# A hybrid decoder layer in fp32 on one core: the gate weights' split kept in DRAM by the first block of tokens and loaded by the other three

## What is computed

```
mod = silu(c) @ W_ada + b_ada              -> shift, scale, gate for two sub-layers
h   = RMSNorm(x) * (1 + scale1) + shift1
proj = h @ W_in    (attention q,k,v | DeltaNet q,k,v | beta | decay | out gate z | branch gate A | branch gate B)
A   = sliding-window attention (window 128, 8 heads, 2 kv heads, QK norm, partial rotary, sinks)
B   = gated DeltaNet (4 heads of 128, short conv, chunked triangular inverse, running state)
merged = sigmoid(gA) * (A @ W_branch[A]) + sigmoid(gB) * (B @ W_branch[B])
x   = x + gate1 * (merged @ W_out)
x   = x + gate2 * SwiGLU(RMSNorm(x) * (1 + scale2) + shift2)     hidden width 2816
```

## Time and profile before

| | |
|---|---|
| median of 3 runs | 3077.72 us (3077.09 to 3078.48) |
| profiled execution | 3072.56 us, its span 3070.8 us |
| busy VectorE | 1632.6 us, 53% |
| busy ScalarE | 1202.7 us, 39% |
| busy GpSimd | 113.2 us, 4% |
| moved | 358.22 MB, mean 117 GB/s |
| SP's queue | 33.8% of the 16 DMA engines' span |
| ScalarE's queue | 8.39 MB, 0.7% |

### The profile page before, as it was taken

How to read it: one execution, slowest core, us unless ns; L and a number is a source line. 1 busy time by engine, 2 the same in 40 slices (tenths; PEclk the granted TensorE clock), 3 DMA queues, 4 the chain that set the end, 5 groups by cost and what they waited for, 6 DMA issues and landing times.

```text
span 3070.8 us, 40245 instructions
## 1 busy us (share of the span) xinstructions
PE 3012.7 (98%) x16056; PEld 2526.0 (82%) x16056; DVE 1632.6 (53%) x2636; ACT 1202.7 (39%) x1969; POOL 113.2 (4%) x109
## 2 busy tenths in 40 slices
PE   7999999999999999999999999999999999999999
PEld 6897878888898788888889878888888978878887
DVE  7876675433566667333365756633336475643333
ACT  3555533222355544222234545422224455432222
POOL 0011000000001100000000110000000011000000
PEclk9999999999999999999999999999999999999999
DMA  6533343222433333222233244322233333322223
GB/s 255 186 127 93 134 162 146 96 96 98 135 111 113 105 129 116 98 103 96 96 131 124 95 118 142 103 96 96 96 100 134 125 110 100 124 82 96 96 96 103
DMA packets 137146, 358.22 MB, mean 117 GB/s; under 512 B 38144, under 2 KB 38272, under 8 KB 135040
## 3 DMA queue, kind: packets, MB, share of 16 engines
q1 hardware_dynamic: 132608, 347.27, 33.8%
q10 hardware_dynamic: 4352, 8.39, 0.7%
HBM read 326.25 MB, written 29.36 MB: 116 GB/s over the span
## 4 chain that ended last, share of the span: by engine, by line
PE 82%; DVE 8%; issue 4%; ACT 2%; DVEq 2%; DMA 1%; SPq 1%; POOL 0%; POOLq 0%; ACTq 0%
PE gb L1702 64%; PE gb L1719 7%; PE gb L2028 4%; PE mb L1873 2%; DVE tmp_c L1412 1%; DVE inv_c L1415 1%; DVE w_lo L1132 1%; PE mb L1846 1%; ACT sc L912 1%; DVE ada_sum L1123 1%; PE mb L1868 1%; PE mb L1788 1%; ACT sc L904 1%; DVE n_acc L1139 1%; DVE nf L1151 1%
## 5 line engine op out<-in xcount | busy, mean ns | idle before, releaser
L740 ACT ACTIVATE w_hi<-w_raw 128x1024 fp32r<-128x1024 f32 x492 | 518.8, 1057 | 1053.5 <-PE gb L1702 977.4
L1702 PE MATMUL gb<-h_hi,w_hi 128*128 128x512 f32 x2336 | 918.7, 393 | 12.0 <-DVE w_lo L1132 6.6
L1702 PE MATMUL gb<-h_lo,w_hi 128*128 128x512 f32 x2336 | 917.9, 393 | 0.0
L1702 PE MATMUL gb<-h_hi,w_lo 128*128 128x512 f32 x2336 | 917.7, 393 | 0.0
L1132 DVE TENSOR_TENSOR w_lo<-w_raw,w_hi 128x1024 fp32r<-128x1024 f32 x492 | 600.8, 1222 | 491.7 <-ACT w_hi L740 490.3
L1702 PEld LDWEIGHTS gb<-h_hi,w_hi 128*128 128x128 f32 x2336 | 440.5, 189 | 103.5 <-DVE w_lo L1132 8.3
L1702 PEld LDWEIGHTS gb<-h_lo,w_hi 128*128 128x128 f32 x2336 | 440.7, 189 | 96.0 <-issue 6.5
L1702 PEld LDWEIGHTS gb<-h_hi,w_lo 128*128 128x128 f32 x2336 | 440.3, 188 | 91.6
L1702 PE MATMUL gb<-hid_hi,w_hi 128*128 128x512 f32 x704 | 274.0, 389 | 0.0
L1702 PE MATMUL gb<-hid_hi,w_lo 128*128 128x512 f32 x704 | 273.9, 389 | 0.0
L1702 PE MATMUL gb<-hid_lo,w_hi 128*128 128x512 f32 x704 | 273.9, 389 | 0.0
(11 more groups left out here) (268 smaller groups left out, 3446.8 us busy)
## 6 DMA issues: line engine op xcount, KB each, us to landing
w_raw<-in_wstream SPq DMA_DIRECT2D x492, 512.0 KB, 3.2
ada_buf<-in_ada_w SPq DMA_DIRECT2D x9, 2048.0 KB, 8.3
x<-in_x SPq DMA_DIRECT2D x4, 2048.0 KB, 10.0
out<-x ACTq DMA_DIRECT2D x16, 512.0 KB, 2.9
ada_buf<-in_ada_w SPq DMA_DIRECT2D x6, 1024.0 KB, 14.8
xs<-in_x SPq DMA_DIRECT2D x12, 512.0 KB, 5.5
scratch_nt<-st_nt SPq DMA_DIRECT2D x16, 256.0 KB, 2.4
scratch_at<-st_at SPq DMA_DIRECT2D x16, 256.0 KB, 2.9
```

The lines of the kernel that those rows point to most:

```text
L740: act.activation(w_hi[s][:, :], w_raw[s][:, :], ACT.Copy).then_inc(w_high.sem, 1)
L1702: last = pe.matmul(bank(j), w, r, start=(i == 0), stop=(i == n - 1))
```

## The change

In block 0 the gate units are split as before, and after VectorE's half is done ScalarE stores the pair (hi, lo; 1 MB) to a DRAM tensor, at the start of its split of the next unit. In blocks 1 to 3 the gate units are neither loaded raw nor split: ScalarE, in the place of its split, waits for the slot and issues the load of the kept pair straight into `w_hi`/`w_lo`; VectorE skips them, and TensorE waits for that load. All other units are split as before; their counts are recomputed. w_hi[s] and w_lo[s] become the halves of one tile.

```diff
+def is_kept(g):
+    b, u = divmod(g, U_PER)
+    return 0 < b < NB and U_GATE <= u < U_BRANCH
+def splits(g):
+    return sum(not is_kept(i) for i in range(min(g, len(UNITS))))
+def loads(g):
+    return sum(not is_kept(i) for i in range(g % RING, g, RING))
+def same_place(g):
+    return max(i for i in range(g % RING, g, RING) if not is_kept(i))
+def kept_loads(g):
+    return sum(is_kept(i) for i in range(g % RING, g + 1, RING))
...
-    w_hi = [sb(f"w_hi{s}", [P, UW], fp32r) for s in range(RING)]
-    w_lo = [sb(f"w_lo{s}", [P, UW], fp32r) for s in range(RING)]
+    w_pair = [sb(f"w_pair{s}", [P, 2, UW], fp32r) for s in range(RING)]
+    w_hi, w_lo = [[w_pair[s][:, i, :] for s in range(RING)] for i in range(2)]
...
+    kept = nc.dram_tensor("scratch_w", (2 * KD, P, 2, UW), fp32, kind="Internal").ap()
...
+    w_kept = [sig(f"w_kept{s}", 0) for s in range(RING)]
+    kept_in = [sig(f"kept_in{s}", 0) for s in range(RING)]
...
             def load_unit(b, u):
-                sp.wait_ge(w_ready.sem, b * U_PER + (u + 1))
+                g = b * U_PER + u
+                if is_kept(g):
+                    return
+                sp.wait_ge(w_ready.sem, RING + splits(same_place(g) + 1))
...
+            def keep_unit(u):
+                s = u % RING
+                act.wait_ge(w_ready.sem, RING + u + 1)
+                act.dma_start(kept[u - U_GATE], w_pair[s][:, :, :].bitcast(fp32)).then_inc(w_kept[s].sem, 16)
...
             def split(b, u):
-                s = u % RING
-                if b * U_PER + u >= NB * U_PER:
+                s, g = u % RING, b * U_PER + u
+                if g >= NB * U_PER:
                     return
-                act.wait_ge(w_loaded[s].sem, b * w_loaded[s].per + 16 * (u // RING + 1))
+                if b == 0 and U_GATE < u <= U_BRANCH:
+                    keep_unit(u - 1)
                 unit_used(b, u - RING)
+                if is_kept(g):
+                    if b == 1 and u < U_GATE + RING:
+                        act.wait_ge(w_kept[s].sem, 16 * len(range(U_GATE + (s - U_GATE) % RING, U_BRANCH, RING)))
+                    act.dma_start(w_pair[s][:, :, :].bitcast(fp32), kept[u - U_GATE]).then_inc(kept_in[s].sem, 16)
+                    return
+                act.wait_ge(w_loaded[s].sem, 16 * (loads(g) + 1))
+                if b == 0 and U_GATE + RING <= u < U_BRANCH + RING:
+                    act.wait_ge(w_kept[s].sem, 16 * len(range(U_GATE + (s - U_GATE) % RING, u, RING)))
                 act.activation(w_hi[s][:, :], w_raw[s][:, :], ACT.Copy).then_inc(w_high.sem, 1)
...
             def split(b, u):
                 s = u % RING
-                if b * U_PER + u >= NB * U_PER:
+                g = b * U_PER + u
+                if g >= NB * U_PER or is_kept(g):
                     return
-                dve.wait_ge(w_high.sem, b * U_PER + (u + 1))
+                dve.wait_ge(w_high.sem, splits(g + 1))
...
+            def wait_weights(b, u):
+                g = b * U_PER + u
+                if is_kept(g):
+                    pe.wait_ge(kept_in[u % RING].sem, 16 * kept_loads(g))
+                else:
+                    pe.wait_ge(w_ready.sem, RING + splits(g + 1))
...
-                    pe.wait_ge(w_ready.sem, w_ready.at(b, u + 1))
+                    wait_weights(b, u)
```

## The result

The changed kernel takes **3095.44 us** (3095.05 to 3097.4, 4 runs) beside 3077.4 (3072.83 to 3078.48) for the kernel before on the same chip: a ratio of 1.0063, 95% interval 1.0051 to 1.0076, 18 us slower. The forecast was 3075.1, within 3068 to 3083.

A forecast was written before the change was run, and what follows sets the result against it. TensorE's own time, nearly the whole span, was taken as the bound. Terms: -1.5 (blocks 1 to 3), -2.1 (merge), +1.8 (block 0), -0.8 (clock) = -2.6 us; 3077.7 - 2.6 = 3075.1, range 3068 to 3083.

The forecast's parts named there:

- What bounds it, and the place: TensorE's time is nearly the whole span; only its waits and lower clock, beside attention and DeltaNet, can be won.
- Splits removed: Blocks 1 to 3: without VectorE's splits of units 6 and 7, the triangular sweeps end 1.8 us earlier.
- Unit 8 and the other units: Gate units: a 1 MB load takes 4.9 us; unit 8's wait nearly goes, the others land before use, costing nothing.
- The image chain against the new loads: Blocks 1 to 3: loads of units 9 and 10 meet image writes and `lc_u`; fair sharing costs 1.3 us, bounds 0 and 6.8.
- The rival on the slower side: `lc_u` before L1888, all four blocks: 1 MB loads go ahead of the images; 3090 to 3097 us; chance 0.13.
- one and a half transfers: The slower rival's case of 5 us of transfers ahead of the images in each block: +12.5 us, 3090.
- Clock, -0.8 us: Lower-clock falls of 1.7 and 1.5 us follow TensorE's waits in blocks 1 and 2; half of one was counted as won.
- signs of being wrong: L1888 waits of 5 us and more or below 2, L1702 waits on kept pairs, or a lower clock in new stretches.
- Block 0, +1.8: Block 0: stores of units 8 and 9 meet the image, 1.3 us, plus 0.5; bounds 0 and 6.8 + 1.5.
- the merge's 0.5: Block 0: ScalarE waits for unit 9, VectorE's rotation and merge come 1.5 us late, 1.0 covered by the later image.
- the ScalarE wait: Block 0: ScalarE waits for VectorE's split, exponentials(1,0) 2.5 us late; TensorE stands 0.9 there, 0.9 less for unit 8.
- The merge, -2.1: TensorE's waits of 1.3 and 0.8 us for VectorE's merge (L1427) go, as splits of units 8 to 10 leave: -2.1 us.

The follow-up runs named there:

- e1: The changed kernel, but gate units 9 and 10 split as before in blocks 1 to 3: 3078.58 us, 1.0006 to the kernel before.
- e10: The changed kernel with only gate unit 9 split as before in blocks 1 to 3: 3089.1 us, 1.0043 to the kernel before.
- e11: The changed kernel with only gate unit 10 split as before in blocks 1 to 3: 3088.51 us, 1.0042 to the kernel before.
- e6: The changed kernel with the kept tensor laid out in runs of 1 KB in DRAM instead of 8 KB: 3098.42 us, 1.0071 to the kernel before.
- e4: The changed kernel, all pairs kept, loads of units 8 and 9 earlier, 10 later, block 0's stores of 4, 6, 8, 9 later: 3070.95 us, 0.9983.
- e7: e4 with unit 10's load behind keep_qk(2) and 10 gate matmuls moved to just ahead of level_x(0): 3064.14 us, 0.996 to the kernel before.
- e2: The changed kernel with block 0 storing all pairs but nothing loaded, blocks 1 to 3 splitting all units: 3084.7 us, 1.0023 to the kernel before.
- e5: The changed kernel with the kept tensor laid out in runs of 4 KB in DRAM instead of 8 KB: 3096.19 us, 1.0064 to the kernel before.

## Why the prediction was wrong

**What bounds it, and the place** were right: the gain and the loss were decided between the last sweep and the first level product.

**Splits removed: right.** In block 1 the sweeps end 1.77 us earlier; 1.76 was forecast.

**Unit 8 and the other units: right in effect.** No wait for a kept pair, though a load takes 6.4 us and not 4.9. It was issued earlier than I had it (below). TensorE arrives 2.6 us earlier at the image, not 1.7.

**"The image chain against the new loads", 1.3 us: this is the step that failed.** It measured 4.4 us a block, 2.2 for each transfer (e1, e10, e11). The fair sharing that it assumed did not take place: 20 packets of SP's queue passed in 2.5 us beside the load, 1353 without it. I had read the DMA share of 0.41 as room, and shared the bandwidth fairly between `lc_u` and one load; the load of unit 9 against the image *writes* I had priced with nothing but an issue. The writes' own bandwidth was no measure: they stood still behind the load, SP's issues were stretched, and the chain is made of 17 of them end to end, which I had read from the earlier trace rows myself. Both loads also went out earlier than I had placed them and so met the writes: unit 9 beside the transpose and not behind it, 2.1 us earlier; unit 10 15.3 us after the copy of the scores, where 18.2 was forecast. With both my bounds in hand (0 and 6.8) I went near the lower one for the weight load that had left SP's queue behind `lc_u`. It was worth 0.5 us at most: from the issue of `lc_u` to the level product it is 4.0 us before and 3.6 in e1, where that load is gone too.

**The rival on the slower side** named this place and its price: it decided from 3.4 us a block, 4.4 were measured, and its formula gives 4 x 4.4 - 7.5 = +10.1 us of waits, beside +9.2 read from the trace. It was given 0.13. That its "one and a half transfers", 3090, come near the measured 3095 is in part luck: it has 5 us a block and nothing for the clock. The rule of the Trainium skill ("DMA: Bandwidth & Descriptors", Queues, rings and completion order: turns by whole packets of some 9 to 17 descriptors) spoke for it. A load here is 8 runs of 8 KB on each engine, which by this rule is one turn. The changed kernel agrees (the writes stood behind whole loads). e6 has 64 runs on each engine; by the typical size that is several turns, though the same section puts the ceiling of a packet at 64 descriptors, by which it would still be about one. More writes did get in beside one of its loads (590 packets, above), and the wait was no shorter.

**Clock, -0.8 us: wrong in sign and size.** In every block the lower level came with the longer wait: 12 to 16 of the 24.8 us of the profiled execution. The prediction had named this among its signs of being wrong and put no price on it. That the waits bring the lower level was not separated by a run of its own; e4 beside e7 shows only that the two go together.

**Block 0, +1.8: 7 to 8 was measured (e2).** The image was the right place; the merge's 0.5 did not show (no such wait in block 0); the ScalarE wait cancelled, as forecast, 0.6 us each way where 0.9 was forecast.

**The merge, -2.1: right**, the wait is gone in blocks 2 and 3, in e4 as well.

## What to carry to other kernels

Before a transfer is moved to another queue, lay its place over every chain of small DMAs that something waits for: 1 MB there cost 2.2 us a block, in the other places tried here nothing that could be measured. A chain that is bound by its issues is not protected by free bandwidth, so price a collision by the whole transfer in front, not by a fair share. And when a change makes a wait longer, ask at once what the clock does during and after it; ahead of an unavoidable wait put work that comes later anyway.

## What was not expected of the hardware

- While a 1 MB transfer of ScalarE's queue was under way, SP's *issue* instructions took longer: groups of four went from 1.9 to 4.4 us, the longest single one to 2.43 us, and writes already issued stood still (20 packets in 2.5 us, 1353 before). Runs of 4 or 1 KB in place of 8 did not shorten it (e5, e6); other sizes of the transfer were not tried.
- A DMA that stands behind an ACTIVATE in ScalarE's order did not wait for its end: the load of unit 9 was issued at 1022.14, the transpose ahead of it ran from 1022.13 to 1024.27; that of unit 10 was issued at 1025.99, before two ACTIVATEs that stand ahead of it in the program began (1026.48, 1026.95). So such a load starts earlier than the place of a compute instruction suggests, which here put both on the image writes.
- The kernel before varies with its clock: in the runs beside e10, 3072.18 us at a mean clock of 0.996 and 3080.49 at 0.992. A time of this kernel without its clock says little below 0.3%.
